# The first microseconds of a two-block transformer kernel on one core: split first load, shared rounding, two tiles of value weights moved ahead, and another source for the warm-up

## The reference, cut to what matters

```
h = rmsnorm(x, attn_norm_w)
proj = h @ w_in            # 1024 x 3072
q_a, k_a, v_a, ... = split(proj)   # q_a and k_a: columns 0 to 511; v_a: columns 512 to 767
```

## Time and profile before

| what | value |
|---|---|
| median of 3 runs | 685.64 us (685.49 to 685.88) |
| the profiled execution | 685.88 us |
| its span, first to last instruction | 683.7 us |
| busy share of PE, DVE, ACT, POOL | 99%, 73%, 61%, 15% |
| weight loads of PE (PEld) | 85% |

### The profile page before, as it was taken

One profiled execution on the slowest core, in us unless ns is written; L12 is line 12 of the kernel. 1 busy time (PEld: TensorE's weight loads), 2 busy tenths in 40 slices (PEclk: granted clock), 3 DMA queues, 4 the chain that ended last, 5 costly groups with the idle time before them and its releaser, 6 DMA issues.

```text
span 683.7 us, 9309 instructions
## 1 busy us (share of the span) xinstructions
PE 675.6 (99%) x3708; PEld 579.6 (85%) x3708; DVE 500.1 (73%) x757; ACT 416.1 (61%) x711; POOL 100.9 (15%) x159
## 2 busy tenths in 40 slices
PE   9999999999999999999999999999999999999996
PEld 8888888888888888888878888888888888888885
DVE  6878787667666666667996776777868877777774
ACT  7787775755555555547446856665576755555553
POOL 3122030788301000011650000000000000000001
PEclk9999999999999999999999999999999999999999
DMA  9936534736555555535445325356453655555401
GB/s 343 398 126 221 210 123 164 274 125 246 185 189 189 196 199 197 198 126 215 161 177 216 126 101 201 139 192 230 162 208 124 241 190 185 185 188 189 178 0 62
DMA packets 19483, 126.12 MB, mean 184 GB/s; under 512 B 2416, under 2 KB 2544, under 8 KB 5232
## 3 DMA queue, kind: packets, MB, share of 16 engines
q1 hardware_dynamic: 19296, 125.34, 49.9%
q10 hardware_dynamic: 144, 0.20, 0.1%
HBM read 124.48 MB, written 1.05 MB: 184 GB/s over the span
## 4 chain that ended last, share of the span: by engine, by line
PE 94%; DVE 5%; POOL 0%; issue 0%; ACT 0%; POOLq 0%; DVEq 0%; ACTq 0%
PE bank L454 91%; PE bank L462 3%; DVE wlo L1507 2%; DVE turned L1507 1%; DVE turned L1888 1%; POOL kt L2014 0%; DVE both L1507 0%; DVE both L1515 0%; DVE xres L1507 0%; POOLq L2214 0%; DVE last L1507 0%; ACT last L1049 0%; ACT junk L1046 0%; ACT both L1049 0%; POOL ss L2019 0%
## 5 line engine op out<-in xcount | busy, mean ns | idle before, releaser
L1507 DVE TENSOR_TENSOR wlo<-raw,whi 128x1024 fp32r<-128x1024 f32 x222 | 275.8, 1253 | 41.5 <-ACT whi L1049 38.3
L1049 ACT ACTIVATE whi<-raw 128x1024 fp32r<-128x1024 f32 x222 | 230.7, 1051 | 2.8 <-PE bank L454 1.7
L454 PE MATMUL bank<-xb,whi 128*128 128x512 f32 x592 | 146.5, 392 | 0.0
L454 PEld LDWEIGHTS bank<-xb,whi 128*128 128x128 f32 x592 | 108.3, 188 | 20.6
L454 PE MATMUL bank<-xa,whi 128*128 128x512 f32 x432 | 108.1, 392 | 0.0
L454 PEld LDWEIGHTS bank<-xa,whi 128*128 128x128 f32 x432 | 79.3, 188 | 15.6
L454 PEld LDWEIGHTS bank<-xb,wlo 128*128 128x128 f32 x592 | 76.3, 191 | 3.1
L454 PE MATMUL bank<-xb,wlo 128*128 128x256 f32 x592 | 77.3, 283 | 0.0
L454 PE MATMUL bank<-whi,hh 128*128 128x512 f32 (+1 forms) x180 | 69.3, 385 | 0.0
L454 PE MATMUL bank<-wlo,hh 128*128 128x512 f32 (+1 forms) x180 | 69.2, 384 | 0.0
L454 PE MATMUL bank<-whi,hl 128*128 128x512 f32 (+1 forms) x180 | 69.2, 384 | 0.0
(11 more groups left out here) (255 smaller groups left out, 826.3 us busy)
## 6 DMA issues: line engine op xcount, KB each, us to landing
raw<-in_w_dram SPq DMA_DIRECT2D x109, 1024.0 KB, 4.8
first<-in_first_dram SPq DMA_DIRECT2D x8, 388.0 KB, 6.1
raw<-in_w_dram SPq DMA_DIRECT2D x4, 512.0 KB, 8.5
bias<-in_bias_dram SPq DMA_DIRECT2D x1, 1024.0 KB, 8.5
xres<-in_x_dram SPq DMA_DIRECT2D x1, 1024.0 KB, 8.3
gain<-in_ffn_norm_w_dram SPq DMA_DIRECT2D x1, 512.0 KB, 9.1
gain<-in_mix_norm_g_dram SPq DMA_DIRECT2D x1, 512.0 KB, 9.9
gain<-in_ffn_norm_g_dram SPq DMA_DIRECT2D x1, 512.0 KB, 5.1
```

Of the source, the lines that this page charges most:

```text
L454: return e.matmul(o, l, r, start=start, stop=stop)
L1049: return e.activation(o, i, ACT.Copy, **options)
L1507: return e.tensor_tensor(out=o, in0=a, in1=b, op=op)
```

## The change

The DMA of tile k = 0 is split: x and gains (264 columns, 132 KB) first, with a semaphore of their own, then the 512 weight columns (256 KB). After tile 1 the first half of unit 4 (512 columns, 256 KB: the value weights of tiles 0 and 1) is loaded, ahead of tile 2; the load of unit 4 further back keeps the other half. For k = 0 ACT rounds the first 256 weight columns and DVE the others, behind its low part of x. Unit 4 is rounded in two halves by ACT and DVE, the first right behind tile 1, the second behind tile 7. On PE a helper `values(half)` does unit 4 in two halves of 12 matmuls: one right behind tile 1, one where `group_1(1, 0)` stood. The warm-up takes a constant 1.0 that is set ahead of the program, read with step 0, in place of `ones`; it waits for nothing, and there are 8 products in place of 9.

```diff
-WARM = 9
+WARM = 8
@@ SyncE
-        for k in range(KT):
+        e.dma_start(first[:, 0, 0:XT], T["first"][0][:, 0:XT]).then_inc(s_x0, 16)
+        e.dma_start(first[:, 0, XT:XT + 512], T["first"][0][:, XT:XT + 512]).then_inc(s_first[0], 16)
+        e.dma_start(first[:, 1, :], T["first"][1]).then_inc(s_first[1], 16)
+        e.dma_start(raw_of(4)[:, 0:512], T["w"][0][:, 0:512]).then_inc(s_early, 16)
+        for k in range(2, KT):
             e.dma_start(first[:, k, :], T["first"][k]).then_inc(s_first[k], 16)
         e.dma_start(vec[:, :], T["vec"]).then_inc(s_vec, 16)
         for u in range(4, 8):
-            o = slice(u % 2 * UNIT, u % 2 * UNIT + UNIT)
-            e.dma_start(raw_of(u), T["w"][u // 2 - 2][:, o]).then_inc(s_unit[u], 16)
+            o = slice(u % 2 * UNIT + (512 if u == 4 else 0), u % 2 * UNIT + UNIT)
+            e.dma_start(raw[u // 2 % NR][:, o], T["w"][u // 2 - 2][:, o]).then_inc(s_unit[u], 16)
@@ TensorE
-        w.wait_ge(*dve.of("ones"))
+        constant = nc.const_aps.tensor(1.0, (128, 128))
         for _ in range(WARM):
-            mm(pb[6][:, 0:128], ones[:, :], ones[:, :], True, True)
+            mm(pb[6][:, 0:128], constant, constant, True, True)
+        def values(half_):
+            w.wait_ge(*dve.of("lo", 4, half_))
+            for t in range(2):
+                for k in (2 * half_, 2 * half_ + 1):
+                    x, c = slice(t * 128, t * 128 + 128), slice(k * 256, k * 256 + 256)
+                    m = mm3(pb[2 + t][:, 0:256], xa_h[:, k, x], xa_l[:, k, x], whi[4][:, c], wlo[4][:, c], k == 0, False)
+            return m
+
         for k in range(KT):
...
             w.wait_ge(*act.of("hi", u, i))
+            if k == 0:
+                w.wait_ge(*dve.of("hi", 0, 0))
...
+            if k == 1:
+                values(0)
...
-        group_1(1, 0)
+        values(1).then_inc(*pe.done("free", 4))
@@ ScalarE
-            w.wait_ge(s_first[k], 16)
+            if k == 0:
+                w.wait_ge(s_x0, 16)
+            else:
+                w.wait_ge(s_first[k], 16)
             copy(xa_h[:, k, :], first[:, k, 0:256], scale=first[:, k, 256:257]).then_inc(*act.done("xhi", k))
-            copy(whi[u][:, half_cols(i)], first[:, k, XT:XT + 512]).then_inc(*act.done("hi", u, i))
-        hi_to(4)
+            if k == 0:
+                w.wait_ge(s_first[0], 16)
+                copy(whi[0][:, 0:256], first[:, 0, XT:XT + 256]).then_inc(*act.done("hi", 0, 0))
+            else:
+                copy(whi[u][:, half_cols(i)], first[:, k, XT:XT + 512]).then_inc(*act.done("hi", u, i))
+            if k == 1:
+                w.wait_ge(s_early, 16)
+                copy(whi[4][:, 0:512], raw_of(4)[:, 0:512]).then_inc(*act.done("hi", 4, 0))
+        w.wait_ge(*landed(4))
+        copy(whi[4][:, 512:1024], raw_of(4)[:, 512:1024]).then_inc(*act.done("hi", 4, 1))
@@ VectorE
             low_gain(xa_l[:, k, :], first[:, k, 0:256], first[:, k, 256:257], xa_h[:, k, :]).then_inc(*dve.done("xlo", k))
+            if k == 0:
+                w.wait_ge(s_first[0], 16)
+                e.tensor_copy(whi[0][:, 256:512], first[:, 0, XT + 256:XT + 512]).then_inc(*dve.done("hi", 0, 0))
+                w.wait_ge(*dve.now())
...
             low(wlo[u][:, c], first[:, k, XT:XT + 512], whi[u][:, c]).then_inc(*dve.done("lo", u, i))
-        lo_to(4)
+            if k == 1:
+                w.wait_ge(*act.of("hi", 4, 0))
+                low(wlo[4][:, 0:512], raw_of(4)[:, 0:512], whi[4][:, 0:512]).then_inc(*dve.done("lo", 4, 0))
+        w.wait_ge(*act.of("hi", 4, 1))
+        low(wlo[4][:, 512:1024], raw_of(4)[:, 512:1024], whi[4][:, 512:1024]).then_inc(*dve.done("lo", 4, 1))
```

More of the change, by code:

```diff
@@ L381, in two_block_program @@
     s_raw = [semaphore(f"raw{i}") for i in range(NR)]
+    s_x0 = semaphore("x0")
+    s_early = semaphore("early")
     s_first = [semaphore(f"first{k}") for k in range(KT)]
@@ L1042, in scalar @@
         w = Waits(e)
-        ready = {"unit": 4}
+        ready = {"unit": 5}
         def op(o, i, f, **options):
```

## The result

The changed kernel takes 686.80 us (median of 22 runs, 685.83 to 687.34) against 685.75 us (22 runs, 685.08 to 686.27) for the kernel before: a ratio of 1.0015, 95% interval 1.0009 to 1.0021. It is about 1 us slower, under the 1.37 us that the prediction called measurable, though with this many runs clear of no change, and outside its range of 684.8 to 686.1. The profiled execution took 686.62 us, 0.74 more than that of before.

The account below looks back on a forecast made before the run. PE's work was taken to bound the kernel, with the low clock holding it back at the start. Starting 0.27 us earlier gave 0.14 off 685.88, 685.74; carried to the median, 685.5 us, range 684.8 to 686.1; the early half saved nothing.

Parts of the forecast that it names:

- the path of the sum: At the start: ACT's x 3.2 to 3.71, DVE's low part to 4.30, then DVE's copy, done at 4.65.
- S: Start of PE's first real matmul: 4.97 before the change, forecast 4.7, bounds 4.6 and 5.45.
- the rival of the pause: PE idle from 4.3 to 4.7 restarts the clock's count; rise at 10.4, end 1.55 us later, 687.2 us; chance 0.12.
- sum: 0.14: PE starts 0.27 us earlier at the low pace, worth 0.14 us at the upper pace, with the clock rising at 6.82.
- the prediction said of a gain: Behind the loop, transposes have 1 us of room before waiting for DVE's scaling; a gain under that passes on.
- value weights ahead: Early 256 KB ahead of tile 2 lands at 5.97 to 6.45, ready by 7.9; 1.44 us of matmuls moved, not removed.
- The rivals: Clock rises in warm-up, 684.9 us (0.17); pause holds it down, 687.2 (0.12); tile 0's pieces land together, 685.9 (0.13).
- PE waiting for tile 2: Behind the early half: a sign of being wrong; tile 2 was forecast rounded by 8.9 to 9.4, without a gap.

Follow-up runs that it names:

- the run above: The changed kernel as it is, run again beside the one with the early load in an array of its own: 687.01 us, ratio 1.0016 to the kernel before.
- the run with ACT alone: Changed kernel with the early load in an array of its own, and tile 0's 512 weight columns rounded by ACT without DVE: 685.69 us, one run.
- the run with the whole unit: Changed kernel with all of unit 4 (512 KB, pieces of 4 KB in steps of 8 KB) loaded at the early load's place: 686.47 us.

## Why the prediction was wrong

**What held.** The first piece landed at 2.89 and the weights at 4.00 (taken: 3.2 and 3.9; 2.89 is under the lowest bound, 3.16). The start was set by DVE's half, at 4.78 (taken: 4.7, bounds 4.6 and 5.45), but not by the path of the sum: DVE had the low part of x at 3.93, not 4.30, and its copy began at 4.02, when the weights were there. The copy took 0.61 us where I took 0.35, so that the two errors nearly cancel; that S came out is in part luck. The clock rose at 6.8, in spite of a pause of 0.2 us between warm-up and work: the rival of the pause, the one that ended slower, didn't happen, and the kernel was slower for another reason. The 0.19 us of earlier start at the low pace were worth 0.12 us by the beginning of tile 1 (sum: 0.14). The loop over k behind the early half went at full pace, and the loss passed through to the end, as the prediction said of a gain.

**The step that failed** is the price of the early load in "value weights ahead": "It lands at 5.97 to 6.45". It landed at 7.84: 2.6 us behind tile 1 instead of 0.70 to 1.18. I priced it from the rate of the stream and from the landings of `first`, whose rows lie one behind the other; the load that I priced takes 2 KB out of each 8 KB. The rows of before with steps of 8 KB were the loads of units 4 to 7, in pieces of 4 KB, later in the queue and at full rate, and they wouldn't have shown it either. The bounds were taken from rows of another layout, so they were no bounds. What the step was worth is shown by the contiguous array: with it the load lands at 5.93 and 6.10, PE doesn't wait, and the loss is gone.

**The rivals** had no case for it. The one mechanism that decided, a transfer put ahead that is late itself and makes the in-order PE wait, was named only as "PE waiting for tile 2" among the signs of being wrong. A rival "the early load comes late" would have had its place (PE behind tile 1, with nothing else to do), its point (a landing after 7.2, since the rounding takes 1.4 and PE is there at 8.56), and a price of about 1 us for each us after that (landing at 7.84, it cost 0.71).

**The median** lost 1.05 us, the profiled pair 0.74. Both profiled executions had a late rise of the clock, at 6.8. Where it rises with the first real matmuls, the changed kernel gains nothing from it: PE then waits 0.84 and 1.02 us for loads, as the run above shows, and its early half still starts at 9.46. That the kernel before, which waits for less, does gain from it is argued; no profile of it with an early rise is at hand. Kernels that wait for little point that way: with the early load contiguous, the profiled executions took 685.36 and 685.32 us where the clock rose at 4.7 and 5.4, and 685.69 in the run with ACT alone, where it rose at 6.8. It could account for the rest; this is not shown.

## What to carry to other kernels

Price a moved load by rows with its own layout and its own place in the queue, not by the mean rate; where there are none, it has no upper bound from the trace (the longest gap between two landings among the first loads of before, 1.79 us, was still short of 2.61), and a late landing is a rival of its own, priced by what the engine that has nothing else to do behind it will pay. Work that is pulled ahead to fill a hole needs its data to be there before the hole, and whatever stands behind its load is late as well. If a small piece of an array must come early, lay it out contiguously.

## What the runs showed that was not expected

- 256 KB as 128 pieces of 2 KB landed 0.68 to 0.86 us behind the load ahead of it when contiguous, 0.70 with steps of 4 KB, and 2.2 to 3.0 us with steps of 8 KB in the first 8 us of the kernel (five runs), while the DMA engines counted as busy for 73% or more of the stretch from 5 to 6 us and moved 104 to 164 GB/s.
- The clock rose at another place in nearly every profile of these kernels, from 3.6 to 6.9 us after the start of the span, with the warm-up starting at 0.83 to 1.11. The Trainium skill, page "TensorE: Matmul & The Clock Gate", Part 1 (The HAM clock gate), says that the watching window runs freely and that the place differs from run to run, by 500 ns to either side; the profiles agree that it differs, but spread over 3.3 us. Two profiles of the changed kernel alone have it at 6.8 and 4.8. It may be part of the 1.2 us between the lowest and the highest run of the kernel before; that is not shown.
- After an early rise and waits of 0.8 and 2.1 us the granted clock went back to 0.50 from 10.5 to 13.8 us. Eight matmuls of 512 columns at 0.427 in place of 0.228 us are 1.6 us: here the waits cost more than their length.
- DVE's copy of 256 columns to fp32r took 0.29 to 0.35 us in most runs and 0.57 to 0.61 in three; in these three GpSimd's cast of `blk_r` just before took 0.53 to 0.58 us, in the others with DVE's copy 0.29. But in the run with the whole unit GpSimd's cast took 0.58 and DVE's copy 0.29, so the one doesn't make the other. What does was not tested.
